# Hybrid mixer block: the second stick-breaking pair's projections and the memory rows in buffers of their own, with a new order of work

## The chip, the cores and the metric

The kernel runs on one core of a Trainium2 chip. The metric is device time in microseconds (us). The kernel before took 1142.4 us, the median of 3 runs (1142.38 to 1142.9). TensorE is called PE in the profile (PEld is its weight load), VectorE DVE, ScalarE ACT, GpSimd POOL; SP issues the DMAs.

## The reference, cut to what matters

One layer on 1024 tokens of width 1024, in float32. RMS norm and one input projection (1024 to 3904 columns) feed four token mixers of 256 channels (4 heads of 64), each with a SiLU gate; then the output projection, a cross-attention to 256 memory rows, and a last norm.

```
h = rms_norm(x, norm_mix);  p = h @ w_in
y_a = rwkv7(p_a)                # r, k, v, decay: recurrence over 1024 tokens
y_b = conv31(val * sigmoid(glu)), layer norm, swish
y_c = hgrn2(q, f, i)            # chunks of 64
y_d = stick_breaking(q, k, v)   # strictly causal, blocks of 128 queries
x = x + concat(y * silu(gate)) @ w_out
mn = rms_norm(mem, norm_mem);  k = mn @ wk;  v = mn @ wv
x = x + softmax((rms_norm(x) @ wq) @ k.T / 16) @ v @ wo
out = rms_norm(x, norm_final)
```

## The kernel before, in words

Activations are kept transposed (channels on the 128 partitions, tokens along the row). Each mixer's 256 channels are two *pairs* (two heads, 128 channels each), numbered 0 and 1.

**Input projection.** It is cut into tiles of 128 output channels, named by mixer, pair and part: ("rw", 0, "k"), ("h", 1, "f"), ("s", 1, "q") and so on. A tile is two halves of 512 tokens; a half is 8 pieces (one per 128 inputs) of 3 matmuls each, high and low parts in fp32r (L1039 to L1041). SP loads a tile's weights (L828), POOL splits them (L962, L963), and ACT or DVE reads the finished bank out (`proj`).

**Mixers.** Each is a chain of stages: the RWKV pairs 0 and 1 and then the HGRN pairs 0 and 1 follow one another, since they share the buffer `A` (13 rows of 1024 tokens); their small matmuls stand at L1090. An HGRN pair has, among others, six levels (`hlev`) of two halves, each with DVE differences and products, an ACT exponential and a PE batch. The convolution is 62 taps on DVE (L1665 on `yT`). Stick-breaking runs pair 0 and then pair 1, in 12 units each: `sbz` (scores, L1306, three passes on ACT, then DVE L1665, L1973, L1662), `sbt` (transpose, L1319, and an exponential on ACT), `sbv` (times the values, L1334); `sbo` closes each half of a pair.

**Buffers.** The stick-breaking q, k, v of both pairs go to the same rows 0, 1 and 3 of `B`, so the tiles ("s", 1, q/k/v) wait for ("sbo", 0, 1), the end of pair 0: once in the planner (`want`, L247) and once on ACT (L1452). The memory's rows, its gain (`MEM_GAIN`, a broadcast of 128 rows) and the square's throw-away row stand in rows of `A` that HGRN pair 0 uses, so they come after ("hfin", 0), the end of HGRN pair 0. The transposed memory rows (`mT`) and all the memory's tiles (mk, qa, mv, vo, L1066 to L1079) overlie the activations, so they wait until every input tile is done.

**Order.** `mixer_order` writes one order of all stages, and every engine follows it in program order. It is a list planner with estimated costs. At each step it chooses between the heads of eight chains (RWKV 0, RWKV 1, HGRN 0, HGRN 1, convolution, stick 0, stick 1, memory) and the next projection piece, by `IDLE` times the PE's idle time plus each other chain's delay times its weight in `URGENT`. Which tile comes next is the lowest `TILE_RANK` among those that may start; `HOLD` keeps a tile or stage back until a named stage is done. The projection pieces are the work that fills PE while the chains wait for DVE and ACT. After the mixers come the three wide products (L1358 to L1360), whose order the change leaves alone.

Of the kernel before, what the change touches and what calls it, by code (L numbers as in the profile page):

```python
# [64 lines left out]
TILE_RANK = {t: n for n, t in enumerate((  # L65
# [6 lines left out]
HOLD = {('h', 1, 'f'): ('sbv', 0, 1, 5)}  # L72
# [46 lines left out]
def mixer_chains():  # L119
# [102 lines left out]
def mixer_order():  # L222
# [24 lines left out]
    for w in "qkv":  # L247
        want("s", 1, w, after=[("sbo", 0, 1)])
# [6 lines left out]
    for i in range(2):  # L255
# [202 lines left out]
def program(nc, x, mem, w_in, w_out, wq, wk, wv, wo, lora, chan, norms, fconst, mconst, out, keys_dram, vals_dram):  # L458
    with ExitStack() as ctx:
# [40 lines left out]
        late = sb("late", [P, 5, T])  # L500

# [119 lines left out]
        mem_at = min(first_mem, tiles_begun(("hfin", 0)) + 2)  # L621
# [177 lines left out]
        MEM_GAIN, MEM_JUNK, MEM_ROWS = 3, 5, 11  # L799
# [1276 lines left out]
```

## Time and profile before

| | us |
|---|---|
| median of 3 runs | 1142.4 |
| the profiled execution | 1140.49 |
| its span | 1138.7 |
| PE busy | 1066.4 (94%) |
| DVE busy | 603.9 (53%) |
| ACT busy | 393.3 (35%) |
| POOL busy | 283.2 (25%) |
| mean granted PE clock | 0.973 of full speed |

The busy time is of one engine over the whole span. In a table by stretch the columns are: the stretch and its length, busy time of PE, PEld, DVE, ACT and POOL with the number of instructions in brackets, the granted PE clock, the share of the DMA engines and GB/s. In a list in order of time each line has the start, the duration, the engine, the kernel's line, what is written from what, the count, and in brackets the idle time before it with what ended that.

### The profile page before, as it was taken

What the parts mean: (1) busy time and instruction counts of PE and PEld (TensorE: products, weight loads), DVE (VectorE), ACT (ScalarE), POOL (GpSimd) and SP (SyncE); (2) the same over time, 40 slices, a digit from 0 to 9 for tenths busy, and PEclk for the clock granted to TensorE, in tenths of its full rate; (3) what the DMA queues carried; (4) which work ended last, traced back from release to release, by engine and by line L of the source; (5) the groups of instructions that cost most, each with busy time, mean ns of one, the idle gap of its engine ahead of it and who ended that gap; (6) DMA issues with size and microseconds to landing.
All of it is one profiled execution on the core that took longest, in us unless ns stands there. A gap on an engine that the chain in (4) does not pass through costs nothing.

```text
span 1138.7 us, 25033 instructions
## 1 busy us (share of the span) xinstructions
PE 1066.4 (94%) x10748; PEld 913.1 (80%) x10748; DVE 603.9 (53%) x857; ACT 393.3 (35%) x695; POOL 283.2 (25%) x259
## 2 busy tenths in 40 slices
PE   7999988999899899999886999999989999999997
PEld 6777867876677698788775778888569999999997
DVE  6337998873447633354685765434323165446115
ACT  7305111114544211445543535444531063123033
POOL 3344621011134200222201100343052233432220
PEclk9899989999899899999988999999999999999999
DMA  6111110000011000111101005856661111111103
GB/s 234 38 28 47 47 28 22 3 21 20 18 38 37 20 4 3 38 37 37 57 2 48 11 2 150 249 167 185 203 206 37 47 38 38 57 57 38 38 20 149
DMA packets 84144, 71.69 MB, mean 63 GB/s; under 512 B 4097, under 2 KB 72897, under 8 KB 84034
## 3 DMA queue, kind: packets, MB, share of 16 engines
q1 hardware_dynamic: 84034, 70.09, 20.3%
q8 instruction: 85, 1.39, 0.5%
q14 instruction: 25, 0.20, 0.1%
HBM read 57.49 MB, written 12.58 MB: 62 GB/s over the span
## 4 chain that ended last, share of the span: by engine, by line
PE 67%; DVE 21%; ACT 6%; DMA 2%; issue 2%; POOL 1%; SPq 0%; DVEq 0%; ACTq 0%; POOLq 0%
PE units L1090 8%; PE bank L1039 7%; PE bank L1358 7%; PE bank L1360 7%; PE bank L1359 7%; PE bank L1040 6%; PE bank L1041 6%; DVE yT L1665 6%; PE bank L1079 4%; DVE A L1662 3%; ACT B L1379 2%; DVE B L1973 2%; PE duo L1306 2%; ACT A L1379 2%; PE bank L1074 1%
## 5 line engine op out<-in xcount | busy, mean ns | idle before, releaser
L1358 PE MATMUL bank<-vhi,act_hi 128*128 128x256 f32 x704 | 199.3, 283 | 0.3 <-DVE x L1996 0.3
L1360 PE MATMUL bank<-vhi,act_lo 128*128 128x256 f32 x704 | 197.6, 281 | 0.0
L1359 PE MATMUL bank<-vlo,act_hi 128*128 128x256 f32 x704 | 197.5, 281 | 0.0
L1039 PE MATMUL bank<-act_hi,whi 128*128 128x512 f32 x464 | 196.7, 424 | 0.0
L1040 PE MATMUL bank<-act_lo,whi 128*128 128x512 f32 x464 | 185.2, 399 | 0.0
L1041 PE MATMUL bank<-act_hi,wlo 128*128 128x512 f32 x464 | 185.0, 399 | 0.0
L1090 PEld LDWEIGHTS units<-A 64*64 64x64 f32 x4608 | 147.2, 139 | 37.7 <-issue 21.3
L1090 PE MATMUL units<-A 64*64 64x64 f32 x4608 | 155.3, 224 | 22.3 <-DVE A L1821 11.7
L962 POOL TENSOR_SCALAR whi<-wraw 128x512 fp32r<-128x512 f32 x62 | 53.8, 867 | 484.4 <-PE bank L1041 387.5
L1358 PEld LDWEIGHTS bank<-vhi,act_hi 128*128 128x128 f32 x704 | 133.1, 189 | 0.4 <-issue 0.4
L1359 PEld LDWEIGHTS bank<-vlo,act_hi 128*128 128x128 f32 x704 | 133.3, 189 | 0.0
L1360 PEld LDWEIGHTS bank<-vhi,act_lo 128*128 128x128 f32 x704 | 132.7, 188 | 0.0
L1039 PEld LDWEIGHTS bank<-act_hi,whi 128*128 128x128 f32 x464 | 88.7, 191 | 25.8 <-issue 4.0
L1041 PEld LDWEIGHTS bank<-act_hi,wlo 128*128 128x128 f32 x464 | 88.4, 190 | 21.8
L1040 PEld LDWEIGHTS bank<-act_lo,whi 128*128 128x128 f32 x464 | 88.9, 192 | 18.0 <-issue 0.7
L963 POOL TENSOR_TENSOR wlo<-wraw,whi 128x512 fp32r<-128x512 f32 x62 | 99.7, 1608 | 5.2
L1665 DVE SCALAR_TENSOR_TENSOR yT<-yT,chn 128x1023 f32<-128x1023 f32 (+30 forms) x62 | 87.4, 1409 | 2.2
L1996 DVE TENSOR_TENSOR x<-x,bank 128x256 f32<-128x256 f32 x64 | 27.0, 422 | 114.9 <-PE bank L1360 114.5
L1665 DVE SCALAR_TENSOR_TENSOR B<-duo,B 128x1024 f32<-128x1024 f32 (+3 forms) x24 | 23.0, 958 | 117.7 <-ACT B L1379 117.6
L947 POOL TENSOR_SCALAR vhi<-vraw 128x512 fp32r<-128x512 f32 x48 | 30.1, 626 | 209.5 <-PE bank L1360 152.9
L1379 ACT ACTIVATE A<-A 128x256 f32<-128x256 f32 (+2 forms) x92 | 55.2, 600 | 59.5 <-DVE A L1662 26.1
L1662 DVE TENSOR_TENSOR A<-A 128x256 f32<-128x256 f32 (+2 forms) x92 | 67.8, 736 | 12.4 <-ACT A L1379 9.4
(181 smaller groups left out, 1621.2 us busy)
## 6 DMA issues: line engine op xcount, KB each, us to landing
wraw<-in_w_in SPq DMA_DIRECT2D x62, 256.0 KB, 2.8
A<-in_x SPq DMA_DIRECT2D x8, 512.0 KB, 7.4
x<-in_x SPq DMA_DIRECT2D x8, 512.0 KB, 8.0
moved<-in_wq SPq DMA_DIRECT2D x16, 256.0 KB, 4.9
keys_dram<-moved SPq DMA_DIRECT2D x16, 256.0 KB, 2.7
vals_dram<-moved SPq DMA_DIRECT2D x16, 256.0 KB, 3.4
vraw<-in_w_out SPq DMA_DIRECT2D x16, 256.0 KB, 2.9
vraw<-keys_dram SPq DMA_DIRECT2D x16, 256.0 KB, 2.6
```

Source lines behind the costliest of these rows:

```text
L962: done(pool, nc.gpsimd.tensor_scalar(hi, raw_view[slot], 1.0, 1.0, ALU.mult, ALU.mult), "w_hi")
L963: done(pool, nc.gpsimd.tensor_tensor(lo, raw_view[slot], hi.bitcast(F32), ALU.subtract), "w_split")
L1039: mm(bank, wh, act_hi[:, k, cols], start=k == 0, stop=False)
L1040: mm(bank, wh, act_lo[:, k, cols], start=False, stop=False)
L1041: ins = mm(bank, wl, act_hi[:, k, cols], start=False, stop=k == KT - 1)
L1090: ins = mm(bank[r, c * CH:(c + 1) * CH], a(r, col), b(r, col), start=n == 0, stop=n == len(terms) - 1)
L1358: mm(bank, ah, vhi[:, (m + 1) % 2, k, :], start=k == 0, stop=False)
L1359: mm(bank, ah, wide_lo(m)[:, k, :], start=False, stop=False)
L1360: ins = mm(bank, al, vhi[:, (m + 1) % 2, k, :], start=False, stop=k == KT - 1)
L1379: return nc.scalar.activation(out, in_, func, **kw)
L1662: ok(V.tensor_tensor(out, a, b, op), name)
L1665: ok(V.scalar_tensor_tensor(out=out, in0=a, scalar=s, in1=b, op0=op0, op1=op1), name)
```

## The change: what it does, and the diff

1. A new buffer `qk1` holds q and k of stick-breaking pair 1, and its v goes to `raw`, the row that the RWKV tiles pass through before their token shift. The tiles ("s", 1, q/k) have no wait of their own any more (but `HOLD` gives them one), ("s", 1, "v") waits for the RWKV pair 1 tiles k, r, v. The wait for the end of pair 0 moves to `sv(1)`, which turns the values into `B` row 2.
2. The memory rows use row 8 for the square and may be normalized after ("rfin", 1), the end of RWKV pair 1, and before the HGRN pair 0's `tok hk`. The gain is no longer loaded as 128 rows: it comes as 8 columns of `chn` and is multiplied in by DVE when it reads the transposed rows (`mT`), which ACT did before.
3. `IDLE`, `URGENT`, `AHEAD`, `TILE_RANK` and `HOLD` have new values.

```
-IDLE = 60.0
-URGENT = (34.211, 64.887, 39.81, 53.8, 25.403, 0.241, 7.449, 7.673)
-AHEAD = 2.956
+IDLE = 27.32
+URGENT = (9.221, 13.454, 23.922, 5.605, 0.665, 0.103, 0.069, 1.256)
+AHEAD = 2.497
 TILE_RANK, after:
+    ('h', 0, 'i'), ('rw', 0, 'r'), ('h', 0, 'f'), ('rw', 1, 'r'), ('rw', 0, 'k'),
+    ('h', 0, 'q'), ('rw', 0, 'gate'), ('h', 1, 'f'), ('cv', 0, 'glu'), ('rw', 1, 'k'),
+    ('s', 0, 'gate'), ('h', 1, 'q'), ('s', 1, 'k'), ('cv', 0, 'val'), ('rw', 1, 'gate'),
+    ('cv', 1, 'gate'), ('h', 1, 'gate'), ('s', 1, 'gate'), ('s', 1, 'q'), ('s', 0, 'v'),
+    ('cv', 1, 'glu'), ('rw', 1, 'v'), ('cv', 1, 'val'), ('h', 1, 'i'), ('rw', 0, 'v'),
+    ('h', 0, 'gate'), ('s', 0, 'q'), ('cv', 0, 'gate'), ('s', 1, 'v')
-HOLD = {('h', 1, 'f'): ('sbv', 0, 1, 5)}
+HOLD = {('s', 1, 'k'): ('hlev', 1, 4, 0), ('s', 1, 'q'): ('mk3', 'ak', 0, 1),
+        ('h', 1, 'gate'): ('hkv', 0, 1), ('h', 0, 'gate'): ('hlev', 0, 2, 0),
+        ('h', 1, 'f'): ('hlev', 0, 3, 1), ('rw', 0, 'gate'): ('sbz', 0, 0, 1),
+        ('sv', 1): ('sbv', 0, 1, 2), ('h', 1, 'q'): ('mk3', 'rk', 1, 1)}
 mixer_order:
-        want("s", 1, w, after=[("sbo", 0, 1)])
+        want("s", 1, w, after=[("proj", "rw", 1, t, 1) for t in "krv"] if w == "v" else ())
-    mem = [(("mn", 0), [("AE", 1.7), ("D", 1.3)], [("hfin", 0)]), ...
-           (("mT", 0), [("P", 0.9), ("A", 1.2)], [("mn", 0)] + all_in),
+    mem = [(("mn", 0), [("AE", 1.7), ("D", 1.1)], [("rfin", 1)]), ...
+           (("mT", 0), [("P", 0.9), ("D", 1.4)], [("mn", 0)] + all_in),
 buffers and waits:
+        qk1 = sb("qk1", [P, 2, T])
+        def sb_in(p, what):
+            if p:
+                return raw[:, 1:1 + T] if what == "v" else qk1[:, "qk".index(what), :]
+            return B[:, {"q": 0, "k": 1, "v": 3}[what], :]
-        MEM_GAIN, MEM_JUNK, MEM_ROWS = 3, 5, 11
+        MEM_JUNK, MEM_ROWS = 8, 11
-                sp.wait_ge(sem("h_done"), 1)
-                sp.dma_start(A[:, MEM_GAIN, :], norms[NORM_MEM:NORM_MEM + 1, :].broadcast_to([P, D])).then_inc(...)
 ACT, proj of "s":
-                    if kind[1] and h == 0:
-                        so.wait_read(act, ("o", 0, 1))
+                    if kind[1] and what == "v":
+                        act.wait_ge(sem("shift_done"), len(shifted))
 ACT, sv:
+                if p:
+                    so.wait_read(act, ("o", 0, 1))
 DVE:
-                stt(rows, rows, stat[:, 72 + i:73 + i], A[:, MEM_GAIN, :], MUL, MUL, "m_scaled")
+                ts(rows, rows, stat[:, 72 + i:73 + i], None, MUL, name="m_scaled")
+            def mT(i):
+                for q in range(2):
+                    bank = pj.rd_open(dve, ("mT", i, q))
+                    each = c0("mg", 4 * q, 4).unsqueeze(2).broadcast_to([P, 4, P])
+                    pj.rd_done(dve, V.tensor_tensor(memT[:, 4 * q:4 * q + 4, i * P:(i + 1) * P], bank, each, MUL),
+                               ("mT", i, q))
```

## Rows read from the trace of the kernel before

**Rows 1.** The page: busy time by engine, and the chain that ended last, by engine.
```profile
PE 1066.4 (94%) x10748; PEld 913.1 (80%) x10748; DVE 603.9 (53%) x857; ACT 393.3 (35%) x695; POOL 283.2 (25%) x259
PE 67%; DVE 21%; ACT 6%; DMA 2%; issue 2%; POOL 1%; SPq 0%; DVEq 0%; ACTq 0%; POOLq 0%
```

**Rows 2.** The table by stretch, columns as in the section above.
```profile
157.00:247.00 90.00, 81.89 (x1834) 70.76 (x1835) 79.76 (x95) 13.46 (x31) 4.94 (x4) 0.97 0.03 9
378.00:441.00 63.00, 59.68 (x1661) 56.44 (x1663) 27.68 (x52) 11.68 (x28) 0.71 (x1) 0.95 0.03 8
...
556.00:600.00 44.00, 34.04 (x560) 29.84 (x559) 36.49 (x61) 18.38 (x36) 3.78 (x4) 0.84 0.01 1
...
613.70:629.00 15.30, 5.73 (x35) 4.96 (x34) 9.41 (x8) 7.74 (x10) 3.77 (x4) 0.59 0.38 104
...
640.00:676.00 36.00, 32.87 (x488) 25.21 (x486) 26.95 (x50) 12.05 (x27) 3.82 (x4) 1.00 0.01 2
...
693.00:829.00 136.00, 132.54 (x926) 107.61 (x928) 58.04 (x61) 65.00 (x96) 34.32 (x33) 1.00 0.61 190
...
855.00:1138.70 283.70, 275.36 (x2335) 274.34 (x2333) 118.03 (x251) 71.12 (x187) 78.27 (x80) 0.99 0.16 51
```

**Rows 3.** PE in order of time, 612 to 633 us.
```profile
612.64 1.09 PE L1334 MATMUL bank<-B 128*64 128x128 f32 x16
622.14 1.97 PE L1319 MATMUL duo<-fcst,B 128*128 128x128 f32 x8 [8.41 <-DVE B L1662]
625.28 1.98 PE L1334 MATMUL bank<-B 128*64 128x128 f32 x16 [1.16 <-ACT B L1379]
627.18 1.97 PE L1138 MATMUL units<-fcst,A 128*128 128x128 f32 x8
628.80 0.78 PE L1039 MATMUL bank<-act_hi,whi 128*128 128x512 f32 x1
...
632.23 0.39 PE L1039 MATMUL bank<-act_hi,whi 128*128 128x512 f32 x1
632.46 0.40 PE L1040 MATMUL bank<-act_lo,whi 128*128 128x512 f32 x1
```

**Rows 4.** DVE in the same stretch.
```profile
618.23 2.60 DVE L1973 TENSOR_TENSOR_SCAN B<-fcst,B 128x512 f32<-128x512 f32 x2
620.86 1.23 DVE L1662 TENSOR_TENSOR B<-duo,B 128x1024 f32<-128x1024 f32 x1
...
628.39 0.69 DVE L1979 TENSOR_TENSOR yT<-yT,bank 128x512 f32<-128x512 f32 x1
```

**Rows 5.** PE in order of time, 561 to 601 us: HGRN pair 0's levels, then single pieces.
```profile
561.73 3.61 PE L1090 MATMUL units<-A 64*64 64x64 f32 x64 [3.01 <-DVE A L1662]
...
570.68 1.98 PE L1090 MATMUL units<-A 64*64 64x64 f32 x32 [0.62 <-DVE A L1821]
573.08 6.02 PE L1090 MATMUL units<-A 64*64 64x64 f32 x96 [0.42 <-DVE A L1821]
579.39 1.15 PE L1090 MATMUL units<-A 64*64 64x64 f32 x32 [0.29 <-DVE A L1821]
...
594.94 1.03 PE L1138 MATMUL units<-fcst,A 128*128 128x128 f32 x8
...
599.87 0.50 PE L1039 MATMUL bank<-act_hi,whi 128*128 128x512 f32 x1
600.21 0.40 PE L1040 MATMUL bank<-act_lo,whi 128*128 128x512 f32 x1
600.45 0.40 PE L1041 MATMUL bank<-act_hi,wlo 128*128 128x512 f32 x1
600.77 1.15 PE L1090 MATMUL units<-A 64*64 64x64 f32 x32
```

**Rows 6.** PE at the start of RWKV pair 0's chain.
```profile
157.78 3.68 PE L1090 MATMUL units<-centre,A 64*64 64x64 f32 x64 [5.07 <-DVE A L1665]
```

**Rows 7.** Groups of instructions: busy, mean ns of one, then idle time before.
```profile
L1421 ACT COPY A<-units 128x512 f32<-128x512 f32 x20 | 11.7, 587 | 43.2 <-PE units L1090 24.9 <-PE units L1236 18.2
L1853 DVE TENSOR_TENSOR A<-units,fcst 128x512 f32<-128x512 f32 x12 | 8.3, 692 | 4.1 <-PE units L1090 4.0
```

**Rows 8.** The same view of DVE, shapes apart, 620 to 640 us.
```profile
L1665 DVE SCALAR_TENSOR_TENSOR A<-A,stat 128x1024 f32<-128x1024 f32 x2 | 2.6, 1284 | 5.5 <-ACT stat L1379 5.5
L1669 DVE TENSOR_SCALAR A<-A 128x1024 f32<-128x1024 f32 x1 | 0.7, 694 | 1.5 <-ACT A L1379 1.5
```

**Rows 9.** The chain that ended last, its first pieces of the memory's tiles: start, us, what.
```profile
695.88 1.49 PE bank L1079 x6
```

More of the change, by code:

```diff
@@ L60 @@
 SWITCH = 0.17
-IDLE = 60.0
-URGENT = (34.211, 64.887, 39.81, 53.8, 25.403, 0.241, 7.449, 7.673)
-AHEAD = 2.956
+IDLE = 27.32
+URGENT = (9.221, 13.454, 23.922, 5.605, 0.665, 0.103, 0.069, 1.256)
+AHEAD = 2.497
 PIECES_TOGETHER = 1
 TILE_RANK = {t: n for n, t in enumerate((
[6 rows of a table removed]
-HOLD = {('h', 1, 'f'): ('sbv', 0, 1, 5)}
[6 rows of a table added]
+HOLD = {('s', 1, 'k'): ('hlev', 1, 4, 0),
+        ('s', 1, 'q'): ('mk3', 'ak', 0, 1),
+        ('h', 1, 'gate'): ('hkv', 0, 1),
+        ('h', 0, 'gate'): ('hlev', 0, 2, 0),
+        ('h', 1, 'f'): ('hlev', 0, 3, 1),
+        ('rw', 0, 'gate'): ('sbz', 0, 0, 1),
+        ('sv', 1): ('sbv', 0, 1, 2),
+        ('h', 1, 'q'): ('mk3', 'rk', 1, 1)}
 def sb_units(th):
@@ L178, in mixer_chains @@
         halves(rec, ("tok", "hk", i), [("P", 0.55), ("A", 1.5)])
+        if i == 0:
+            rec[-2] = rec[-2][:2] + (rec[-2][2] + [("mn", 1)],)
+            rec[-1] = rec[-1][:2] + (rec[-1][2] + [("mn", 1)],)
         halves(rec, ("hkv", i), [("P", 1.1), ("D", 2.2)], lambda h: [("tok", "hk", i, h)])
@@ L259, in mixer_order @@
     needs[("xw",)] = []
-    mem = [(("mn", 0), [("AE", 1.7), ("D", 1.3)], [("hfin", 0)]), (("mn", 1), [("AE", 1.7), ("D", 1.3)], []),
-           (("mT", 0), [("P", 0.9), ("A", 1.2)], [("mn", 0)] + all_in),
-           (("mT", 1), [("P", 0.9), ("A", 1.2)], [("mn", 1)])]
+    mem = [(("mn", 0), [("AE", 1.7), ("D", 1.1)], [("rfin", 1)]), (("mn", 1), [("AE", 1.7), ("D", 1.1)], []),
+           (("mT", 0), [("P", 0.9), ("D", 1.4)], [("mn", 0)] + all_in),
+           (("mT", 1), [("P", 0.9), ("D", 1.4)], [("mn", 1)])]
     for n in range(KT):
@@ L620, in program @@
         first_mem, first_move = tiles.index(["mk", 0]), tiles.index(["qa", 0])
-        mem_at = min(first_mem, tiles_begun(("hfin", 0)) + 2)
+        mem_at = min(first_mem, tiles_begun(("rfin", 1)) + 2)
         x2_at = tiles_begun(("hfin", 1)) + 3
@@ L1305, in sbz @@
                     for hd, r in enumerate(heads):
-                        ins = mm(bank[:, hd, c * P:(c + 1) * P], B[r, 0, tb * P:(tb + 1) * P],
-                                 B[r, 1, k0 + c * P:k0 + (c + 1) * P], start=not add, stop=True)
+                        ins = mm(bank[:, hd, c * P:(c + 1) * P], sb_in(p, "q")[r, tb * P:(tb + 1) * P],
+                                 sb_in(p, "k")[r, k0 + c * P:k0 + (c + 1) * P], start=not add, stop=True)
                 sz.pe_post(ins, key)
@@ L1451, in proj @@
                 elif g == "s":
[L1452 to L1459 removed]
+                    if kind[1] and what == "v":
+                        act.wait_ge(sem("shift_done"), len(shifted))
+                    copy_out(pj, key, sb_in(kind[1], what)[:, hs(h)], scale=HD ** -0.5 if what == "q" else None)
                 elif g == "mk":
@@ L2027, in snorm @@
                 ts(p_, p_, soft[:, 3, u:u + 1], None, MUL, name="p_ready" if n == 3 else "dve_step")
-            run({"derive": derive, "xn": xn, "mn": mn, "xT": lambda i: lo_part("xT", i, tn),
+            run({"derive": derive, "xn": xn, "mn": mn, "mT": mT, "xT": lambda i: lo_part("xT", i, tn),
                  "proj": proj,
```

18 lines of the change are left out of this document (6 added, 12 removed), and 7 rows, old and new, of the table TILE_RANK.

## The prediction

> **What bounds the kernel now.** I read the busy shares first: PE is busy 94% of the span, DVE 53%, and the chain that ended last runs 67% through PE and 21% through DVE [rows 1]. So PE is the bound, except where it stands idle. The idle time is in few places, which the table by stretch shows as the length minus PE's busy time [rows 2]: 8.1 us of 157 to 247 us (RWKV pair 0), 3.3 us of 378 to 441 (RWKV pair 1), 10.0 us of 556 to 600 (HGRN pair 0's levels), 9.6 us of 613.7 to 629, 3.1 us of 640 to 676 (HGRN pair 1's levels), and 3.5 us of the 136 us after 693, in which the memory's tiles fill PE. From 855 us on come wide products that this change leaves alone, 283.7 us.
>
> The granted clock fell in two of these stretches, to 0.84 and 0.59 as means: it stood at the lower level, 1.2 GHz, part of the time, each time after PE had been idle or thinly used [rows 2]. What that costs can be read from equal work: 16 matmuls at L1334 took 1.09 us at 612.64 and 1.98 us at 625.28 [rows 3].
>
> The stall at 613.7 us is the sharpest. PE has ended a `sbv` and then waits 8.41 us for the DVE subtraction that ends `sbz` of stick pair 0's last unit, and 1.16 us more for ACT [rows 3]. DVE's scans and that subtraction fill 618.23 to 622.09, and `sbo` follows at 628.39 [rows 4]. No projection piece fills the hole: the three tiles left, ("s", 1, k/v/q), may not start before that `sbo`. The first piece starts at 628.80, in the same half microsecond.
>
> **The change part by part.** The measure of filling work is a tile: matmuls of a piece start 0.23 us apart [rows 3], so one tile (48 matmuls) is 11.2 us of PE.
>
> *A. The tiles of stick pair 1 are free of pair 0.* The stall goes as far as any piece is ready there, and after the change no projection tile is tied to the end of pair 0: the held ones wait for HGRN or RWKV stages only, and the memory's tiles for the input tiles. Gain: 8.41 + 1.16 = 9.6 us idle, and the slow clock: L1334 1.98 against 1.09, L1319 and L1138 1.97 each against 1.03 for the same 8 transposes [rows 3, 5], together 0.89 + 0.94 + 0.94 = 2.8, and the first three matmuls of the tile some 0.6 more. Sum 13.0. Bounds: 0, if the last units of pair 0 again meet no filler, and 13.0. I take 13.0, since a moved hole would be counted where it lands (D, E).
>
> *B. Filler in HGRN pair 0's levels.* By the ranks, the tiles ("h", 0, gate) and ("h", 1, f) may start after levels 2 and 3 and are wanted there; before, no tile was placed in these levels (the hold of ("h", 1, f) was the sixth unit of stick pair 0). DVE is busy 36.5 of the 44 us, so the levels keep their pace and PE's holes can be filled: 10.0 us idle, and from the slow clock 64 matmuls in 3.61 us, 32 in 1.98, 96 in 6.02 against 1.15 us per 32 [rows 2, 5], which is 1.3 + 0.8 + 2.6 = 4.7, part of it hidden under DVE's pace; I count 3.5. Bounds 0 and 13.5. Two tiles are 22.4 us of filler against 13.5 us of loss, but they may not start until level 2, before which the two largest waits lie. I take 8.
>
> Of the clock: the row shows 32 matmuls at 1.15 us and at 1.98 us within 10 us, with idle gaps of only 0.3 to 3.0 us between batches [rows 5]. The Trainium skill (TensorE: Matmul & The Clock Gate, "HAM oscillation — how this bites in real kernels") says that work after a too thin stretch starts at the half clock, so that a schedule pays for a hole twice. By that rule any filler that closes the gaps would win back the slow clock as well, B would be 13.5 and the sum 5.5 us better; by the rows alone, where DVE sets the pace, it stays at 8.
>
> *C. The opening order.* The tiles now go rw r, rw k, cv glu, cv val, and ("rw", 0, "v") falls from the 8th to the 10th place. The taps of the convolution begin one tile (11 us) sooner, and RWKV 0's chain two tiles (22 us) later. So fewer of the 62 taps share DVE with the chain; before, DVE was busy 79.8 of 90 us there and PE idle 8.1 [rows 2], after a wait of 5.07 us for DVE at the chain's first batch [rows 6]. Bounds: gain of all 8.1 + 5.07 = 13.2, or a loss of the whole 22 us (the second rival). I take a gain of 5, that first wait.
>
> *D. HGRN pair 1's levels.* Before, three tiles (33.6 us) lay beside them and PE was idle 3.1 of 36 us. Now ("s", 1, k) is held until level 4 of this pair, and, since the memory's tiles need every input tile done, nothing of the memory can fill either; left are ("h", 1, gate), 11.2 us, and units of stick pair 0. Bounds: loss of 0, and of 10.0 + 3.5 (what the levels of pair 0 lose with no tile) less 3.1, so 10.4. I take 6.
>
> *E. RWKV pair 1.* Its batches alone fill PE to 59.7 of 63 us [rows 2], but the recurrence and the gap at its end want about one and a half tiles, and one is left, ("s", 1, v). At the end, the h tiles wait for ("rfin", 1). Loss: 0 to 6 (one ACT and DVE step as the 5.07 us wait of [rows 6] and its start); I take 2.
>
> *F. Single pieces between float32 batches.* The piece at 599.87 takes 0.90 us to the next batch against 0.70 within a tile [rows 3, 5], 0.2 more. Some ten more such places: 0 to 4, I take 2.
>
> *G. The memory rows.* DVE scales two rows with one operand less, 694 against 1284 ns [rows 8], and multiplies four banks (692 ns each) that ACT copied (587 ns) [rows 7]. That is 1.2 us less and 2.8 more on DVE, 2.3 less on ACT. All of it lies beside memory pieces, where DVE is busy 58 of 136 us [rows 2]; with no cover it would cost 0.4 us for the longer read. The broadcast gain load and SP's wait for HGRN pair 0 in front of it disappear; nothing on PE waited for them, so 0. SP's wait for ("rfin", 1) now stands in front of a weight load two tiles ahead of use; a tile is 11.2 us, so 0. `sv(1)`'s wait on ACT has only later stages behind it, and stick pair 1 could not start sooner in any case: 0.
>
> Sum: -13.0 - 8 - 5 + 6 + 2 + 2 = -16.0 us. The profiled execution, 1140.5 (its span 1138.7 and 1.8 around it), becomes 1124.5; the median of the runs stands 1.9 above it, so the forecast is 1126.4 us. Stick pair 1 sets no tighter bound: its units run inside the 136 us after 693, in which PE is busy 132.5 [rows 2], so PE's work and not this chain fills that stretch, and it starts earlier by what is saved in front of it.
>
> **The rivals.**
> *Only the stall goes.* B, C and the losses cancel: 1142.4 - 13.0 = 1129.4. For it: the holds keep filler from the levels where the largest waits are. It lies inside the forecast's range.
> *The freedom is used fully.* The new order spreads filler so that of the 10.0 + 9.6 + 8.1 + 3.3 + 3.1 = 34.1 us idle only a fifth remains, and the slow clock of A and B (6.9) goes: 27 + 7 = 34 less, 1108. For it: 29 tiles are enough filler in total. Against: DVE-paced stretches whose tiles are held.
> *Slower: the chain becomes the bound.* RWKV 0, RWKV 1, HGRN 0 and HGRN 1 are one serial chain, and ("s", 1, k) is tied to its end by the hold, so stick pair 1 and all memory tiles hang on it. If the chain starts 22 us later and wins back only the 15.3 us of 613.7 to 629 [rows 2] on its way, level 4 of HGRN 1 and all behind it come 7 us later: 1142.4 + 6.7 = 1149. It decides from the point where C's delay exceeds what A, B and freer DVE give the chain. Against it: before, PE-filling tiles stood in the chain's way as well, and these two tiles don't return later.
> *Nothing.* The hold on ("s", 1, k) keeps most of the old order and holes move: 1142.
>
> **How the numbers follow.** Forecast and its near variants (1118 to 1132, with the first rival) 0.53; full use 0.18; nothing 0.06; slower 0.23. A measurement can tell about 0.2% (2.3 us) from no change. Faster: 0.53 + 0.18 = 0.71; same 0.06; slower 0.23. The likeliest case has its own range of 1117 to 1135; the range that should hold 8 in 10 reaches to the full use and to the slower case, 1108 to 1148.
>
> **What would show it.** A: in the changed trace, no PE wait over 2 us for L1662 on B at the end of stick pair 0, and granted clock 1.00 there. B: projection pieces between HGRN 0's level batches, PE idle under 3 us of their 44. C: first batch on `centre` near 180 us with no 5 us wait. D: PE idle and a lower clock in HGRN 1's levels, between its `tok hv` and level 4. E: a PE wait of some us before the first ("h", 0) piece. The forecast is wrong if the memory's first piece comes later than before (695.88 us) [rows 9], or if the sum of idle from 150 to 830 us does not fall.

## The result, and the profile after

| | before | after |
|---|---|---|
| median of the runs, us | 1142.39 (1141.47 to 1142.9, 4 runs) | 1134.88 (1134.36 to 1137.12, 4 runs) |
| ratio after / before, 95% interval | | 0.9945 [0.9927, 0.9962] |
| span of the profiled execution, us | 1138.7 | 1133.2 |
| PE / DVE / ACT / POOL busy, us | 1066.4 / 603.9 / 393.3 / 283.2 | 1065.3 / 605.6 / 390.5 / 293.4 |

By the medians the kernel became 7.5 us faster, in the direction forecast and with less than half of the 16.0 us. The ratio is worth 6.3 us, since other rounds had the kernel before at medians of 1140.7 to 1141.1, and the two profiled executions lie 5.5 us apart, which is what the stretches below add up to. The page of the changed kernel, busy time and the chain that ended last, answers to [rows 1]:

```profile
PE 1065.3 (94%) x10748; PEld 923.5 (81%) x10748; DVE 605.6 (53%) x861; ACT 390.5 (34%) x691; POOL 293.4 (26%) x259
PE 67%; DVE 20%; ACT 7%; issue 2%; DMA 2%; POOL 1%; SPq 0%; DVEq 0%; ACTq 0%; POOLq 0%
```

Shares can't show where the time went, since nothing in them moved. A table by stretch can, if its bounds are events that both kernels have: the first output matmul of RWKV pair 0's recurrence, the same of pair 1, the first batch of HGRN pair 0's levels, of pair 1's, the first piece of the memory's tiles, and the first wide product. The kernel before, cut at these events (length; busy time and count of PE, PE's weight loads, DVE, ACT, POOL; granted clock; DMA share; GB/s):

```profile
150.00:257.35 107.35, 94.96 (x1899) 78.64 (x1897) 90.85 (x108) 16.48 (x35) 13.12 (x11) 0.97 0.07 17
257.35:451.17 193.82, 182.94 (x2504) 147.31 (x2504) 98.60 (x130) 66.15 (x104) 39.92 (x28) 0.96 0.08 21
451.17:556.64 105.47, 105.43 (x734) 82.88 (x733) 43.72 (x47) 52.17 (x64) 27.32 (x28) 1.00 0.17 46
556.64:640.71 84.07, 64.53 (x855) 54.45 (x855) 59.18 (x93) 40.83 (x70) 7.56 (x8) 0.84 0.07 20
640.71:695.81 55.10, 51.16 (x776) 41.55 (x775) 37.71 (x76) 21.06 (x42) 3.82 (x4) 1.00 0.14 40
695.81:838.75 142.94, 139.48 (x888) 109.61 (x887) 60.99 (x63) 68.81 (x101) 42.54 (x40) 1.00 0.59 186
```

The changed kernel, cut at the same events:

```profile
150.00:264.42 114.42, 101.86 (x1935) 87.78 (x1933) 88.55 (x103) 16.25 (x35) 18.61 (x14) 0.94 0.08 21
264.42:471.07 206.65, 197.20 (x2591) 159.14 (x2589) 105.93 (x137) 76.72 (x114) 42.68 (x32) 0.98 0.08 20
471.07:566.26 95.19, 90.06 (x689) 72.69 (x687) 47.14 (x48) 48.19 (x65) 25.27 (x20) 0.95 0.17 45
566.26:635.14 68.88, 62.81 (x822) 51.14 (x821) 46.35 (x84) 33.00 (x58) 11.87 (x12) 0.98 0.07 17
635.14:688.31 53.17, 44.28 (x732) 38.09 (x731) 42.63 (x84) 22.11 (x44) 0.00 (x0) 0.87 0.15 42
688.31:829.29 140.98, 137.88 (x883) 108.96 (x882) 59.42 (x62) 66.56 (x97) 43.49 (x40) 1.00 0.60 188
```

The lengths alone mislead, because the order moved projection pieces across the cuts: before the first cut stand 164 pieces in one kernel and 181 in the other. What can be compared is PE's loss in a stretch: the idle time (length less busy) and the slow clock (length times one less the granted clock, taken from the trace with more digits than the rows print). The two overlap where PE idles at the low clock, so the sum is somewhat too large in both kernels.

| stretch, by its end | before: idle + clock | after: idle + clock | change |
|---|---|---|---|
| 150 us to RWKV 0's recurrence | 12.4 + 3.4 | 12.6 + 6.8 | +3.6 |
| RWKV 1's recurrence | 10.9 + 6.8 | 9.4 + 5.1 | -3.2 |
| HGRN 0's levels | 0.0 + 0.0 | 5.1 + 5.1 | +10.2 |
| HGRN 1's levels | 19.5 + 13.7 | 6.1 + 1.7 | -25.4 |
| first memory piece | 3.9 + 0.0 | 8.9 + 6.8 | +11.8 |
| first wide product | 3.5 + 0.0 | 3.1 + 0.0 | -0.4 |

With -1.0 from 48 to 150 us the losses fall by 4.3 us, from 81.2 to 76.9; all of that is idle time, and the clock's part is 29.0 in both. The fourth line is the large gain, and three others give most of it back. The first wide product starts at 829.29 us in place of 838.75, so 9.5 us were won up to there. The other 5.1 us are busy time: PE is busy 733.4 us from 48 us to there in place of 738.5, for the same work (experiments 5 to 8 show what makes the pieces shorter). The wide products, of which the change touches no instruction, then take 297.2 us from their first to their last matmul in place of 293.1, and lose 4.1 again. Each kernel has one profiled execution, so a difference of a microsecond or two in a line says little.

The stall of [rows 3] is gone. PE in order of time at the end of stick pair 0: the last `sbv` (L1348) runs beside the level batches, and the waits are those of HGRN pair 0's levels:

```profile
566.26 2.08 PE L1104 MATMUL units<-A 64*64 64x64 f32 x64
568.28 1.09 PE L1348 MATMUL bank<-B 128*64 128x128 f32 x16
571.39 3.62 PE L1104 MATMUL units<-A 64*64 64x64 f32 x64 [2.02 <-DVE A L1673]
577.94 1.15 PE L1104 MATMUL units<-A 64*64 64x64 f32 x32 [1.26 <-DVE A L1839]
```

In place of it stand two waits, at the start of RWKV pair 0's chain, which answers to [rows 6], and at that of HGRN pair 1's levels:

```profile
180.00 3.68 PE L1104 MATMUL units<-centre,A 64*64 64x64 f32 x64 [7.88 <-DVE A L1676]
...
641.71 3.68 PE L1104 MATMUL units<-A 64*64 64x64 f32 x64 [4.49 <-DVE A L1673]
```

DVE ahead of the first of them. L1676 on `yT` is a tap of the second convolution, L1680 and L1676 on `A` are the last opening shift of ("rw", 0, "v"), for which PE waits:

```profile
161.29 2.15 DVE L1676 SCALAR_TENSOR_TENSOR yT<-yT,chn 128x994 f32<-128x994 f32 x1
...
165.06 12.78 DVE L1676 SCALAR_TENSOR_TENSOR yT<-yT,chn 128x1023 f32<-128x1023 f32 x8
177.87 0.75 DVE L1680 TENSOR_SCALAR A<-raw,der 128x1024 f32<-128x1024 f32 x1
178.66 1.28 DVE L1676 SCALAR_TENSOR_TENSOR A<-raw,chn,A 128x1024 f32<-128x1024 f32 x1
179.98 1.27 DVE L1676 SCALAR_TENSOR_TENSOR yT<-yT,chn 128x1015 f32<-128x1015 f32 x1
```

Eight taps, 12.78 us, stand in DVE's queue ahead of a shift of 2.0 us. Its input was there at 168.05 us, when ACT had copied the second half of the tile to `raw`. PE has nothing from 172.12 us on, and its granted clock is 0.79, 0.70 and 0.83 in the three stretches of 10 us from 170 on.

### The profile page after: what moved, and what is told of

The parts are those of the page before. It is cut to its first block, busy times and chain, and to the rows that moved or that the text cites. A ratio compares the mean times of both kernels' runs of the same rounds, so it can differ in the third digit from the quotient of the medians.

```text
span 1133.2 us, 25031 instructions
## 1 busy us (share of the span) xinstructions
PE 1065.3 (94%) x10748; PEld 923.5 (81%) x10748; DVE 605.6 (53%) x861; ACT 390.5 (34%) x691; POOL 293.4 (26%) x259
## 4 chain that ended last, share of the span: by engine, by line
PE 67%; DVE 20%; ACT 7%; issue 2%; DMA 2%; POOL 1%; SPq 0%; DVEq 0%; ACTq 0%; POOLq 0%
PE units L1104 11%; PE bank L1372 7%; PE bank L1373 7%; PE bank L1374 7%; DVE yT L1676 6%; PE bank L1053 6%; PE bank L1054 5%; PE bank L1055 5%; PE bank L1093 4%; DVE A L1673 4%; ACT A L1393 2%; PE duo L1320 2%; PE duo L1333 2%; ACT B L1393 1%; DVE A L1676 1%
## 5 line engine op out<-in xcount | busy, mean ns | idle before, releaser
L1053 PE MATMUL bank<-act_hi,whi 128*128 128x512 f32 x464 | 191.5, 413 | 0.0
L976 POOL TENSOR_SCALAR whi<-wraw 128x512 fp32r<-128x512 f32 x62 | 58.6, 944 | 459.3 <-PE bank L1055 312.4
L977 POOL TENSOR_TENSOR wlo<-wraw,whi 128x512 fp32r<-128x512 f32 x62 | 103.2, 1665 | 5.2
L1676 DVE SCALAR_TENSOR_TENSOR yT<-yT,chn 128x1023 f32<-128x1023 f32 (+30 forms) x62 | 92.0, 1484 | 2.2
L1676 DVE SCALAR_TENSOR_TENSOR B<-duo,B 128x1024 f32<-128x1024 f32 (+3 forms) x24 | 23.0, 958 | 110.1 <-ACT B L1393 110.0
```

What stands on the lines that cost most here:

```text
L976: done(pool, nc.gpsimd.tensor_scalar(hi, raw_view[slot], 1.0, 1.0, ALU.mult, ALU.mult), "w_hi")
L977: done(pool, nc.gpsimd.tensor_tensor(lo, raw_view[slot], hi.bitcast(F32), ALU.subtract), "w_split")
L1053: mm(bank, wh, act_hi[:, k, cols], start=k == 0, stop=False)
L1676: ok(V.scalar_tensor_tensor(out=out, in0=a, scalar=s, in1=b, op0=op0, op1=op1), name)
```

## The experiments

Each ratio is to the kernel before, timed on the same chip in the same rounds. Where two experiments are compared, each has its own interval, of about 0.002 to either side.

**1. The buffers and the memory rows alone.** The old weights, holds and edges, with `qk1`, `sb_in`, the gain in `chn` and `mT` on DVE:

```
 old IDLE, URGENT, AHEAD, TILE_RANK, HOLD; old `after=` lists
+        qk1 = sb("qk1", [P, 2, T])
+        def sb_in(p, what): ...
+    ("mg", KT)) in CHAN
-                stt(rows, rows, stat[...], A[:, MEM_GAIN, :], MUL, MUL, "m_scaled")
+                ts(rows, rows, stat[...], None, MUL, name="m_scaled")
+            def mT(i): ...
```

> The changed kernel's buffers, waits and DVE memory-row scaling, with the order of the kernel before, stage by stage the same. Theory (the order alone makes the difference of 7.5 us; buffers and the gain as columns cost nothing, and the ACT wait of stick pair 1 only moves): 1142.4 us, within 1.5. Rival 1 (the shorter memory scaling and the dropped 512 KB load bring part of it): 1139 to 1140. Rival 2 (four reads of the transposed memory rows on DVE instead of ACT delay the stage after them): 1144. The 8.4 us wait of PE at the end of stick pair 0 is there in all three.

Measured: 1.0041 [1.0026, 1.0056], slower. The first memory piece comes at 695.62 us, as before (695.81), and the whole loss lies behind it: the wide products take 298.4 us from their first start to their last end, against 293.4. So the buffers, whose part G in the forecast was 0, cost 5 us in a place whose instructions they don't touch. Experiments 5 to 8 take this up.

**2. The freedom with the old weights.**

```
-IDLE = 27.32
-URGENT = (9.221, 13.454, ...)
-HOLD = {('s', 1, 'k'): ('hlev', 1, 4, 0), ...}
+IDLE = 60.0
+URGENT = (34.211, 64.887, ...)
+HOLD = {('h', 1, 'f'): ('sbv', 0, 1, 5)}
```

TILE_RANK went back too, and SP stores the last memory tiles ahead of its x loads.

> The changed kernel with IDLE, URGENT, AHEAD, TILE_RANK and HOLD of the kernel before: the tiles of stick pair 1 and the memory rows are free, the planner is not retuned (SP stores the last memory tiles ahead of its x loads, since it would wait for HGRN pair 1 before them otherwise). Theory (freedom is no gain in itself: the planner takes any filler that is ready, so the input tiles and then all memory tiles run before HGRN pair 1's levels, and these and stick pair 1 are left with nothing beside them): the stall at 614 us is gone, but some 150 us of chain hold only about 50 us of PE work, so 1200 to 1250 us, with PE idle and the lower clock at the end of the mixers. Rival (PE's work is the bound and filler is filler wherever it stands): 1126 to 1135.

Measured: 1.1015 [1.0989, 1.1041], 114 us slower. The three stick tiles and then the memory's are spent as filler before HGRN pair 1's levels, and behind them stick pair 1 runs with no filler. PE's waits, summed by who is waited for (us in total, times, longest), show it in one line, the softmax chain of stick pair 1:

```profile
PE duo L1327 <- DVE B L1667: 64.2, 11, 8.0
PE units L1098 <- DVE A L1833: 18.9, 25, 1.5
```

In the changed kernel no such waits are left, and there the hold of ("s", 1, "k") keeps the memory's tiles for the stretch that needs them. Since all weights and holds were put back at once, that it is this hold is argued and not shown.

**3. The new weights without the freedom.**

```
-        want("s", 1, w, after=[("proj", "rw", 1, t, 1) for t in "krv"] if w == "v" else ())
+        want("s", 1, w, after=[("sbo", 0, 1)])
-    mem = [(("mn", 0), [...], [("rfin", 1)]), ...
+    mem = [(("mn", 0), [...], [("hfin", 0)]), ...
```

> The changed kernel with its new weights, ranks and holds, but with the old edges for the planner: tiles of stick pair 1 after the end of pair 0, memory rows after HGRN pair 0. The planner then fills HGRN pair 0's levels with ('s',1,'q') and ('h',1,'i'), and leaves RWKV pair 1's chain without any tile. Theory (the new weights with spread filler bring most of the gain, the freedom of ('s',1,'q') and ('s',1,'v') as filler in the RWKV chains the rest): 1136 to 1142. Rival 1 (freedom is what brings it): 1142 to 1150, PE idle in RWKV pair 1's recurrence from about 400 to 490 us. Rival 2 (freedom is not used at all): 1135.

Measured: 1.0215 [1.0193, 1.0238], 1165.4 us, more than any of the three expectations. From RWKV 0's recurrence to RWKV 1's PE loses 26.5 + 13.9 us in place of 9.4 + 5.1, near where the first rival looked for it. Neither half is worth anything without the other; the sum of the parts alone (+0.4%, +10%, +2%) says nothing of the whole (-0.55%).

**4. The held tile through HGRN pair 1's levels.** The 16 pieces of ("s", 1, "k") are set by hand between the level batches in place of behind level 4, and the first memory pieces take the places left (the stages `mT`, `sv(1)` and the first `sbz` of pair 1 move ahead with them):

```
+ plan = [("hdiag", 1, 1)] * 6 + [("hlev", 1, 0, 0)] * 2 + [("hlev", 1, 0, 1)] + ...
+ SCHED = edit_d(schedule())
```

> The changed kernel with one tile moved by hand: ('s',1,'k') stands through the levels of HGRN pair 1 (6 pieces before level 0, then 2, 1, 1...), where it was held until level 4, and the first two memory tiles take its place behind the levels, with sv(1) and mT ahead of them. Theory (term D was too small: from 630 to 660 us PE is idle 8.7 us and at clock 0.66 in two of three slices, since the one tile left was used up before the levels): that idle goes and nothing new comes, 1135 - 7 to 9 = 1126 to 1128 us. Rival 1 (the levels are paced by DVE, so pieces between batches delay them and the idle time comes back behind): 1133 to 1136. Rival 2 (the memory weights, which may only be loaded once that tile has been read, come too late for their new place): 1135 to 1140, with a PE wait for the transfer before the first memory piece.

Measured: 1.0008 [0.9995, 1.0022], 7 us slower than the changed kernel. PE in order of time:

```profile
644.44 1.15 PE L1148 MATMUL units<-A 64*64 64x64 f32 x32 [2.64 <-DVE A L1717]
646.93 1.15 PE L1148 MATMUL units<-A 64*64 64x64 f32 x32 [0.45 <-DVE A L1883]
...
665.69 1.15 PE L1148 MATMUL units<-A 64*64 64x64 f32 x32 [3.16 <-DVE A L1883]
667.79 3.38 PE L1148 MATMUL units<-A 64*64 64x64 f32 x64 [0.95 <-DVE A L1883]
```

The wait of 4.49 us at 641.71 shrinks to 2.64, and 3.16 comes back at 665.69. The first memory piece comes 13.1 us earlier (675.21 against 688.31), but the first wide product 4.6 us later (833.89 against 829.29), and between the two PE is idle for 8.7 us in place of 3.1. That fits memory pieces that were drawn forward and are missing in stick pair 1. None of the expectations reached so far: the worst was 1140 us, and it took 1142.2.

**5 to 8. Where the buffers stand.** The eight new columns of `chn` move all that is allocated behind it by 32 bytes, and `qk1` moves the tiles' and the wide products' buffers by 8192 more. Added up from the sizes of what is allocated ahead of them, `whi` and `vhi` both start at 32 modulo 64 before and at 0 after. `act_hi` and `act_lo` are allocated ahead of `chn` and stay where they were. Four kernels put 32 unused bytes in other places:

```
+        _pad = sb("pad", [P, 8])      # behind qk1 (5), behind chn (6, 7), behind chn and late (8)
```

> The changed kernel with 32 bytes of unused SBUF between qk1 and the buffers behind it; order, waits and instructions are the same. The changed kernel's matmuls follow each other by 0.2271 us in the projection pieces (kernel before 0.2332) and by 0.1200 us in the wide products (kernel before 0.1181). Both buffers of weights and of wide products had moved by an odd number of 32 bytes. Theory (the place of the moving operand in units of 32 bytes sets the spacing): here the projections' weights stay where the changed kernel has them, at 0 modulo 64, and the wide products' buffers go back to their old place modulo 64, so the pieces stay at 0.227, the wide products come down to 0.118, the wide phase takes 293 us in place of 297, and the kernel ends at 1130.5 us, ratio to before 0.990. Rival (the 8 KB by which the buffers moved, or the changed last stages before it, cost the wide phase its 4 us): spacing stays 0.120 and the time 1134.9, ratio 0.9945. Second rival (noise in how the wide phase falls from build to build): another figure altogether.

> The changed kernel with 32 bytes of unused SBUF right behind chn, whose 8 new columns had moved everything behind by 32 bytes: now all buffers stand where the kernel before has them modulo 64, and those behind qk1 8 KB further. Theory (place modulo 64): the pieces go back from 0.2271 to 0.2332 us, 1392 matmuls, of which most on the path: +7 us; the wide products back to 0.118: -4 us; sum about 1137.5, ratio 0.996. Rival (8 KB): pieces and wide products stay at 0.227 and 0.120, 1134.9.

> The kernel before with 32 bytes of unused SBUF right behind chn and nothing else changed. Theory (place modulo 64): its pieces come down from 0.2332 to 0.2271 us and its wide products go up from 0.1181 to 0.1200, as in the kernel with the new buffers alone, whose ratio was 1.0041: the wide phase takes 297.5 us in place of 293 (+4.5), and the pieces give back less than 2 us, since that kernel's first memory piece came no earlier (695.62 against 695.81). So 1145, ratio 1.003 to 1.004. Rival (the 8 KB, or the new waits and the DVE copies of that kernel made it slower): 1142, ratio 1.000.

> The kernel before with 32 bytes of unused SBUF behind chn and 32 more behind late, so that only the weights of the projections change their place modulo 64 and the wide products' buffers do not. Theory (place modulo 64): pieces 0.2275 us apart, wide products 0.1175 to 0.118; the wide phase takes 293 to 295.5 us and the time is that of the kernel before, ratio 0.998 to 1.000, 3 us less than with the one pad (1.0028). Rival (any shift of those buffers against the layout before costs): as with one pad, ratio 1.003.

Spacing is the mean time between the starts of neighbouring matmuls of a piece (512 columns, 1392 of them) and of the wide products (256 columns, 2304), gaps over 0.26 and 0.15 us left out; the phase is from the first wide matmul's start to the last one's.

| kernel | `whi` mod 64 | `vhi` mod 64 | piece, us | wide, us | phase, us | ratio |
|---|---|---|---|---|---|---|
| before | 32 | 32 | 0.2331 | 0.1180 | 293.1 | 1 |
| 7. before, one pad | 0 | 0 | 0.2280 | 0.1197 | 295.7 | 1.0028 [1.0012, 1.0044] |
| 8. before, two pads | 0 | 32 | 0.2279 | 0.1174 | 292.2 | 0.9993 [0.9978, 1.0007] |
| after | 0 | 0 | 0.2275 | 0.1197 | 297.2 | 0.9945 [0.9927, 0.9962] |
| 5. after, pad behind `qk1` | 0 | 32 | 0.2275 | 0.1174 | 295.3 | 0.9925 [0.9910, 0.9939] |
| 6. after, pad behind `chn` | 32 | 32 | 0.2333 | 0.1174 | 295.5 | 0.9925 [0.9899, 0.9951] |

Both spacings follow the place modulo 64 in all six kernels, and the 8 KB change neither: 5, 6 and 8 have the same wide spacing. The 0.1180 of the kernel before lies a little above their 0.1174 with `vhi` at the same place, so that place isn't all of it. The rows of two matmul lines show both effects, with the same order of work; the changed kernel, kernel 5, and kernel 6 (busy us, mean ns):

```profile
L1372 PE MATMUL bank<-vhi,act_hi 128*128 128x256 f32 x704 | 200.4, 285 | 0.1
L1053 PE MATMUL bank<-act_hi,whi 128*128 128x512 f32 x464 | 191.5, 413 | 0.0
```
```profile
L1373 PE MATMUL bank<-vhi,act_hi 128*128 128x256 f32 x704 | 199.2, 283 | 0.0
L1054 PE MATMUL bank<-act_hi,whi 128*128 128x512 f32 x464 | 191.6, 413 | 0.0
```
```profile
L1373 PE MATMUL bank<-vhi,act_hi 128*128 128x256 f32 x704 | 199.2, 283 | 0.0
L1054 PE MATMUL bank<-act_hi,whi 128*128 128x512 f32 x464 | 193.7, 417 | 0.0
```

The wide spacing reaches the time: kernel 7 is slower than the one before and kernel 8 is not, the only difference in spacing being the wide one. That is most of what experiment 1 lost, whose spacings are those of kernel 7 (0.2279 and 0.1197). The piece spacing does not reach it: kernels 7 and 8 have the fast pieces, 5.1 ns x 1392 = 7 us less work, and win nothing, and kernel 6 has the slow ones and is level with kernel 5. Fewer busy us in stretches that wait for DVE come back as idle time or slow clock: the losses of the table above, summed from 48 us to the first wide product, are 76.9 us in the changed kernel and 68.0 in kernel 6, whose first memory piece comes at 687.89 against 688.31. The wait at RWKV pair 0's first batch shows how:

```profile
180.06 3.22 PE L1105 MATMUL units<-centre,A 64*64 64x64 f32 x62 [4.49 <-DVE A L1677]
```

In kernel 6 the batch starts at 180.06 us, in the changed kernel at 180.00; with the faster pieces PE is only sooner at the wait, which is 7.88 us in place of 4.49. The old order has the same: 5.07 us before, 6.33 in kernels 7 and 8 and in experiment 1. In my expectation I gave kernel 6 the 7 us; that was wrong. And the pad gave back 2 of the 4.1 us of the wide phase. Over all runs here the phases of single executions reach from 292.1 to 295.5 us with the fast wide spacing and from 294.9 to 298.2 with the slow one, and what sets that spread I have not found.

**9. The taps later (C).** Taps 3 to 10 lose their places in front of the shift, the others move up, and eight places further on are new:

```
+    for i in at[:8]:      # the first eight places of taps 3 to 30
+        s[i] = None
+    for b in (("mk3", "rb", 0, 0), ("tok", "a", 0, 1), ("xk", 0, 1), ("w2", 0, 1),
+              ("hh", 0, 0), ("gt", 0, 1), ("cs", 0, 1), ("cs", 0, 3)):
+        s.insert(s.index(b) + 1, "tap")
```

> The changed kernel with taps 3 to 10 of the second convolution taken out of their places before RWKV pair 0's last opening shift and spread behind it; the instructions are the same. Changed kernel: PE idle 7.88 us at 172.12 to 180.00 behind DVE, whose shift of (rw, 0, v) stood behind 8 taps of 165.06 to 177.84. Theory (the order put the taps in front of a shift that PE waits for): that wait falls to under 2 us, and what follows keeps 4 to 6 us of it: 1130 us, ratio 0.989 to 0.991. Rival (DVE as a whole is what bounds the opening, the taps only come later and are waited for there): within 1.5 us of the changed kernel, ratio 0.9935 to 0.9955.

Measured: 0.9863 [0.9848, 0.9879], 1125.6 us, 9.3 us faster than the changed kernel, 3 us more than the theory's most. DVE in order of time:

```profile
164.26 2.60 DVE L1692 SCALAR_TENSOR_TENSOR yT<-yT,chn 128x1023 f32<-128x1023 f32 x2
167.38 0.75 DVE L1696 TENSOR_SCALAR A<-raw,der 128x1024 f32<-128x1024 f32 x1 [0.52 <-ACT raw L1451]
168.17 2.20 DVE L1692 SCALAR_TENSOR_TENSOR A<-raw,chn,A 128x1024 f32<-128x1024 f32 x1
```

The shift now runs when its input is there, 10.5 us sooner, and the same stretches as above are:

```profile
150.00:255.22 105.22, 96.90 (x1932) 83.07 (x1930) 88.62 (x102) 16.22 (x35) 18.30 (x14) 1.00 0.09 22
255.22:461.54 206.32, 195.83 (x2590) 158.20 (x2588) 105.95 (x137) 76.69 (x114) 42.67 (x32) 0.98 0.08 20
461.54:556.74 95.20, 89.18 (x689) 71.83 (x688) 46.89 (x47) 48.15 (x65) 24.63 (x20) 0.96 0.17 45
556.74:625.64 68.90, 63.89 (x821) 52.45 (x821) 46.87 (x85) 33.04 (x58) 11.85 (x12) 0.95 0.07 17
625.64:678.78 53.14, 42.92 (x731) 36.87 (x731) 42.62 (x84) 22.10 (x44) 0.00 (x0) 0.90 0.15 42
```

The recurrence starts 9.2 us earlier, and each later event 9.5 us earlier: nothing behind it takes the gain back. The first stretch has as much DVE work (88.62 against 88.55 us) and loses 8.3 + 0 us in place of 12.6 + 6.8. PE's busy time in it falls by 5.0 us for the same matmuls, its idle time by 4.2. So over half of the gain is the clock, 1.00 in place of 0.94. I had priced the idle time alone. The Trainium skill (TensorE: Matmul & The Clock Gate, "HAM oscillation — how this bites in real kernels") says that matmuls behind a long enough idle gap start at the half clock, so that the gap is paid twice; the trace agrees, with 4.2 us of idle time and 5.0 of slower matmuls from one wait of 7.88. How much the clock takes is not fixed: the kernels of experiments 3 and 4 have the same wait of 7.88 us and lose 3.4 us by the clock in that stretch, where the changed kernel and kernel 5 lose 6.8.

**10, 11. Fewer taps, and more (both with the pad behind `qk1`).** Four places given up in place of eight; and eight more taps moved, out of the levels into the recurrence:

```
-    for i in at[:8]:
+    for i in at[:4]:                                  # 10, with four new places
+    for c in (4, 5, 7, 8, 9, 11, 12, 13):             # 11, on top of experiment 9's edit
+        s.insert(s.index(("cs", 0, c)) + 1, "tap")
```

> As the kernel with the taps later and the pad (1121.0 us), but with four taps (3 to 6's places) given up in place of eight, and four new places in place of eight. Theory (PE's wait is the queue of taps ahead of the last opening shift: 7.88 us with eight, of 1.5 to 2.2 us each): four taps less take 6 us from the wait, 2 us of it stay, and the levels behind keep 4 taps fewer of load: 1123.5 us, ratio 0.984 to 0.987. Rival (the gain of 9 us comes from taking taps out of the levels behind, or from the places that they went to, and goes with their number): half of it, 1127 to 1128, ratio 0.988 to 0.989.

> As the kernel with the taps later and the pad (1121.0 us), with eight more taps moved, out of the levels of RWKV pair 0 into its recurrence, where DVE is busy for 4.4 of 15 us. PE is idle for 8.3 us of 157 to 257 with the eight taps moved. Theory (DVE's taps in the levels still delay it there): 2 to 4 us less, 1118 us, ratio 0.979 to 0.982. Rival (the levels' waits are DVE's own chain, and the taps of 1.3 us now stand in front of the recurrence's copies, one of them in about every second step of 1.3 us): level waits as before and new ones in the recurrence, 1123 to 1127 us, ratio 0.984 to 0.988.

Measured: 0.9868 [0.9847, 0.9890] and 0.9847 [0.9822, 0.9871], against 0.9832 [0.9812, 0.9853] for eight taps with the pad (experiment 12). The medians, 1125.9, 1123.7 and 1121.0, lie within overlapping intervals, so here the traces decide. With four taps, PE's first batch:

```profile
174.36 1.85 PE L1120 MATMUL units<-centre,A 64*64 64x64 f32 x56 [2.62 <-DVE A L1692]
```

Four taps less took 5.3 us from the wait of 7.88, 1.3 each, and the recurrence starts at 256.31 against 255.22 with eight and 264.42 with none: 8.1 of the 9.2 us with half of the taps (with eight and the pad it is 256.94). So the queue in front of the shift is what counts, not the load behind it. With sixteen, PE's idle time of 157 to 257 us is 7.9, against 8.3 in kernel 9 and 7.5 in kernel 12, while in 257 to 272, where they have none, it is 1.5: nothing is won in the levels, and the recurrence has no room for taps.

**12. The best of both.** Experiment 9's edit and experiment 5's pad:

> The kernel with the taps of the second convolution later, and 32 bytes of unused SBUF between qk1 and the buffers behind it. Theory (the two effects are independent: the taps are worth 9 us ahead of the memory rows, the place of the wide products' buffers 2 us behind them): 1123.3 us, ratio 0.984 to 0.985; wide matmuls 0.1174 us apart in place of 0.1197, first to last 295.5 us. Rival (the place only takes busy time that the clock or the drain takes back): 1125.5, ratio 0.986.

Measured: 0.9832 [0.9812, 0.9853], 1121.0 us, 19.9 under the 1140.9 of the kernel before in these rounds. The wide spacing is 0.1174, the phase 293.8. This version beats both kernels. What the pad adds on top of experiment 9 is 3 us by the medians, but the two intervals touch.

**13, 14. The other holes (E and D), on top of experiment 9.** The second half of ("s", 1, "v") out of RWKV pair 1's recurrence, behind its last sums; and the first half only of ("s", 1, "k") ahead of HGRN pair 1's levels:

```
+    mine = [("piece", "s", 1, "v", 1, k) for k in range(KT)] + [("proj", "s", 1, "v", 1)]   # 13
+    at = s.index(("var", 1)) + 1
+    mine = [("piece", "s", 1, "k", 0, k) for k in range(KT)] + [("proj", "s", 1, "k", 0)]   # 14
+    at = s.index(("hdiag", 1, 1)) + 1      # six of them, two behind ("hlev", 1, 0, 0)
```

> The kernel with the taps later, and besides with the 8 pieces of the second half of (s, 1, v), which stand in RWKV pair 1's recurrence, put behind its last sums, where PE waits 2.47 us at 481.50 and 1.16 us at 485.07 for the first stick pair's exponentials. Theory E (the recurrence's own chain is shorter than the pieces put in it, so that they delay it, and the wait behind it is open): the waits of 3.63 us are covered and nothing comes up in the recurrence, 1125.6 - 3 = 1122.5 us, ratio 0.983 to 0.984. Rival (the recurrence waits on its own chain once the pieces are gone): each of the steps that lose a piece waits about as long as the piece took, sum zero or worse, 1125 to 1130, ratio 0.986 to 0.990.

> The kernel with the taps later, and besides with the first half of the tile (s, 1, k), 8 pieces of 0.70 us, put ahead of HGRN pair 1's level 0 (6 pieces) and behind its first batch (2), in place of behind level 4. PE waits 4.47 us there at 627.72 for DVE. Theory D (the hold on that tile leaves the level waits bare, and the place behind level 4 needs only half of the pieces): the wait goes, and behind level 4 up to 1.5 us comes back; 1122.5 us, ratio 0.983 to 0.985. Rival (as with the whole tile moved: DVE is the bound of this stage, what PE gains ahead it waits for behind level 4): 1125.5 us or worse, ratio 0.986 to 0.990, with a new wait of 3 us at about 655.

Measured: 0.9868 [0.9845, 0.9892] and 0.9890 [0.9873, 0.9907], against 0.9863 without them. 13 is level with it, 14 slower; neither gains what its theory said. In 13 the wait of 2.47 us is covered, but the first memory piece comes at 682.88 against 678.78, and the recurrence's stretch loses 12.0 + 8.1 us in place of 10.5 + 3.4; its profiled execution, 1130.45 us, is 5 us above its median, so these stretches look worse than most of its runs. In 14 the wait of 4.47 us becomes 2.64, with that stretch at 12.2 + 6.8 in place of 10.2 + 5.1:

```profile
637.56 1.15 PE L1133 MATMUL units<-A 64*64 64x64 f32 x32 [2.64 <-DVE A L1702]
...
677.62 1.22 PE L1133 MATMUL units<-A 64*64 64x64 f32 x18 [3.02 <-issue]
```

The second row is a wait for nothing that the profile shows; kernels 5, 10 and 12 have one of 2.3, 1.6 and 1.74 us in that place and that of 9 none, so I don't put it down to the edit.

So the idle time that DVE's chain leaves in these stretches can be moved about by filler, and I found no place from which it went away.

## Why the prediction was wrong

**A, the stall, and B, filler in HGRN pair 0's levels: right.** The forecast had -13.0 and -8 here. From HGRN 0's first level to HGRN 1's the losses fell by 25.4 us, in a sum that counts twice where PE idles at the low clock. No wait over 2.02 us is left in the levels, and the clock is 0.98 in place of 0.84. As foretold, the waits that remain are those before level 2, where no tile may start.

**C, the opening order: this is the step that failed.** It read: "I take a gain of 5, that first wait." The wait of 5.07 us [rows 6] did not go. It became 7.88, the clock fell behind it, and the losses of the stretch rose by 3.6 us, 8.6 from the forecast. I had argued with DVE's load: fewer taps beside the chain. But PE didn't wait for DVE's load. It waited for one shift, and what stood in front of that shift in DVE's queue is decided by the order, not by the sum. The trace of the kernel before had shown this already. The shift's input was there at 147.79 us, and DVE came to it at 155.65, behind twelve taps:

```profile
135.47 20.14 DVE L1665 SCALAR_TENSOR_TENSOR yT<-yT,chn 128x1011 f32<-128x1011 f32 x12
155.65 0.75 DVE L1669 TENSOR_SCALAR A<-raw,der 128x1024 f32<-128x1024 f32 x1
```

So the changed order did not bring the fault: it put eight taps where twelve had stood, and the shift is 9.8 us late in place of 7.9. How much longer PE waits depends on the buffers too. With the pieces' weights at 32 modulo 64, as before, the wait goes from 5.07 to 4.49 us (kernel 6) and the stretch's losses from 15.8 to 11.9; with them at 0 the wait goes from 6.33 (kernel 7) to 7.88 and the losses from 17.0 to 19.4. So the sign of C is open, by single executions; what all four have is the wait that C took to be gone. Experiment 9 moves the taps, with DVE's busy time unchanged, and gives back 9.3 us; experiment 10 shows in its trace that it is the queue. With C at -5 the losses would have fallen by 12.9 us. The kernel with the taps moved ran in 1125.6, next to the forecast of 1126.4, but that is in part chance: D, E and G came out worse than forecast, A and B better.

**D, HGRN pair 1's levels: right in sign, too small.** Forecast +6, with a bound of 10.4; the losses of the stretch rose by 11.8, beyond the bound. Of this 6.8 is the clock, which I had taken from pair 0's levels at 3.5. The wait at level 0 (4.49 us) is longer than any of pair 0's, 3.01 us before [rows 5] and 2.02 after.

**E, RWKV pair 1, and F: within their bounds.** Forecast +2 each, up to 6 and 4. The two stretches that they touch changed by -3.2 and +10.2, +7.0 together; pieces went from the second to the first. F can't be told apart from E.

**G, the memory rows and buffers: wrong.** I priced it at 0, since its instructions lie beside other work. They do. What I left out is that a new buffer moves all the others: the wide products, the last 297 us with PE full, were issued 0.1197 us apart in place of 0.1180. Experiments 1, 5, 7 and 8 put that at 2 to 5 us. The same shift made the projection pieces faster, which was worth nothing by kernel 8.

The marks set in the prediction read so: A held; B's idle time was 6 and not under 3; C's first batch on `centre` came at 180.00, as said, but with the wait; D held; E held as waits of 2.07 and 1.16 us; the first memory piece came earlier, and PE's idle time from 150 to 830 us fell from 50.3 to 45.2 us. The rival with the chain as the bound (1149) named the right place, C's delay, but priced it too high: the chain starts 22 us later, is 7.1 us later at RWKV 0's recurrence and 5.6 us earlier at HGRN 1's levels.

## What to carry to other kernels

When an order changes, read what stands in the queue of the engine that PE waits for, instruction by instruction, in front of each one that PE needs: a busy share says nothing of it, and a wait of 8 us at one shift cost 9 us of time with the slow clock behind it. A hole is priced as idle time plus the clock behind it. After any change to the buffers, compare the spacing of the matmuls that the change does not touch; if it moved, try a pad of 32 bytes before you look for a cause in the order. And a wait in the kernel before is worth the same reading as one in the changed kernel: here both had it.

## What the runs showed of the hardware

**The place of an operand changes how fast matmuls follow each other.** 32 bytes of shift in SBUF moved the 512-column pieces from 0.2331 to 0.2275 us (the weights at 32 and at 0 modulo 64, the operand loaded into PE) and the 256-column products from 0.1174 or 0.1180 to 0.1197 (the right-hand matrix at 32 and at 0, the operand streamed through PE). The two are fast at opposite places. Six kernels agree. Of what PE itself reads in the pieces only the weights moved, since `act_hi` and `act_lo` stay, so the streamed operand, which the expectation of experiment 5 named, is not it there. Why the place matters isn't shown.

**DVE and POOL slow each other.** A tap takes 1.27 us at 179.98 and 2.15 at 161.29. POOL in the same stretch, splitting weights, has its first operation at 0.62 and at 1.45 us:

```profile
156.67 0.62 POOL L976 TENSOR_SCALAR whi<-wraw 128x512 fp32r<-128x512 f32 x1 [3.59 <-PE bank L1055]
157.38 2.11 POOL L977 TENSOR_TENSOR wlo<-wraw,whi 128x512 fp32r<-128x512 f32 x1
159.57 1.45 POOL L976 TENSOR_SCALAR whi<-wraw 128x512 fp32r<-128x512 f32 x1
```

Of the 62 taps of the changed kernel, 35 ran while POOL did nothing, with a mean of 1.27 us, and 27 beside POOL, with a mean of 1.76; before it was 43 at 1.27 and 19 at 1.73. So the taps took 87.4 us before and 92.0 after. The Trainium skill (SBUF — State Buffer, "SBUF: two separate sides") says that a DVE instruction with two SBUF inputs and a GpSimd instruction that reads SBUF hold a shared port in turn; the longer durations on both sides agree, but no experiment here took the splits away.
